# Issuing every second 4 MB load of the expert weights from ScalarE's DMA queue instead of SyncE's

## What is computed

```
logits = h @ w_router + b_router            # 256 x 32
top_val, top_idx = top_k(logits, 4); gates = softmax(top_val)
for each expert e, on the frames that chose it:
    hu  = xb @ w_up[e] + b_up[e]            # 1024 -> 2048
    act = min(glu, 7) * sigmoid(1.702 * min(glu, 7)) * (clip(lin, -7, 7) + 1)
    y   = (act @ w_down[e] + b_down[e]) * gate
x = x + sum over the chosen experts of y
```

## Time and profile before

| what | us |
|---|---|
| median of 3 executions | 1036.49 (1036.40 to 1037.47) |
| the profiled execution, its own time | 1035.9 |
| span of the profile | 1033.7 |
| PE busy | 997.6 (97%) |
| DVE / ACT / POOL busy | 202.8 / 114.4 / 12.8 |
| DMA | 424.94 MB, mean 411 GB/s |

### The profile page before, as it was taken

One profiled execution on the slowest core, in us unless ns is written; L12 is line 12 of the kernel. 1 busy time (PEld: TensorE's weight loads), 2 busy tenths in 40 slices (PEclk: granted clock), 3 DMA queues, 4 the chain that ended last, 5 costly groups with the idle time before them and its releaser, 6 DMA issues.

```text
span 1033.7 us, 10934 instructions
## 1 busy us (share of the span) xinstructions
PE 997.6 (97%) x4494; PEld 386.7 (37%) x4494; DVE 202.8 (20%) x486; ACT 114.4 (11%) x230; POOL 12.8 (1%) x26
## 2 busy tenths in 40 slices
PE   8999999999999999999999999899998989999998
PEld 4446553434343434333333334232333324232332
DVE  0456132121111211212121211112111211112012
ACT  2426111010000001010101000000000000000000
POOL 0200000000000000000000000000000000000000
PEclk9999999999999999999999999999999999999999
DMA  9955889999999999999999999999999999999996
GB/s 368 400 242 243 368 335 428 433 427 419 432 429 431 435 431 427 434 435 430 431 435 431 427 434 435 430 430 436 431 427 434 435 430 430 436 430 425 432 429 268
DMA packets 22609, 424.94 MB, mean 411 GB/s; under 512 B 3617, under 2 KB 4385, under 8 KB 6721
## 3 DMA queue, kind: packets, MB, share of 16 engines
q1 hardware_dynamic: 22208, 424.17, 96.4%
q10 hardware_dynamic: 384, 0.54, 0.1%
HBM read 423.65 MB, written 1.05 MB: 411 GB/s over the span
## 4 chain that ended last, share of the span: by engine, by line
PE 70%; DMA 28%; another core or an unknown queue 1%; DVE 0%; issue 0%; ACT 0%; POOLq 0%; SPq 0%; POOL 0%; DVEq 0%
PE psum L1433 31%; DMA everything<-in_w_moe 28%; PE psum L1467 15%; PE psum L1090 4%; PE psum L1314 4%; PE psum L1353 4%; PE psum L1223 3%; PE psum L1057 3%; PE psum L1304 2%; PE psum L1065 2%; PE psum L1082 1%; PE psum L1073 1%; PE psum L1362 0%; DMA everything<-in_x_turned 0%; PE psum L1325 0%
## 5 line engine op out<-in xcount | busy, mean ns | idle before, releaser
L1433 PE MATMUL psum<-everything 128*64 128x512 f32 x2048 | 463.7, 598 | 3.6 <-DMA everything<-in_w_moe 3.4
L1467 PE MATMUL psum<-everything 128*64 128x512 f32 x1024 | 227.8, 595 | 22.5 <-DMA everything<-in_w_moe 22.5
L1433 PEld LDWEIGHTS psum<-everything 128*64 128x64 f32 x2048 | 137.9, 136 | 297.3 <-issue 286.4
L1467 PEld LDWEIGHTS psum<-everything 128*64 128x64 f32 x1024 | 72.2, 137 | 164.9 <-issue 148.9
L736 DVE TENSOR_TENSOR everything<-psum,everything 128x512 f32<-128x512 f32 (+1 forms) x38 | 25.0, 663 | 342.8 <-PE psum L1314 332.5
L1022 DVE TENSOR_SCALAR everything<-psum 128x512 f32<-128x512 f32 x32 | 22.1, 692 | 344.9 <-PE psum L1433 344.9
L1314 PEld LDWEIGHTS psum<-everything 128*128 128x128 f32 x480 | 55.8, 191 | 24.3 <-issue 24.3
L1353 PE MATMUL psum<-everything 128*128 128x512 f32 x128 | 64.2, 606 | 0.0
L693 ACT ACTIVATE everything<-everything 128x512 f32<-128x512 f32 x32 | 20.2, 631 | 390.4 <-DVE everything L1022 390.4
L1314 PE MATMUL psum<-everything 128*128 128x128 f32 x480 | 61.5, 281 | 0.0
L1090 PE MATMUL psum<-everything 128*128 128x512 f32 x96 | 42.1, 594 | 0.0
(11 more groups left out here) (158 smaller groups left out, 296.4 us busy)
## 6 DMA issues: line engine op xcount, KB each, us to landing
everything<-in_w_moe SPq DMA_DIRECT2D x80, 4096.0 KB, 43.0
everything<-in_w_moe SPq DMA_DIRECT2D x27, 2048.0 KB, 15.6
everything<-in_w_moe SPq DMA_DIRECT2D x8, 1024.0 KB, 8.4
everything<-in_w_in SPq DMA_DIRECT2D x3, 2048.0 KB, 26.0
everything<-in_w_out SPq DMA_DIRECT2D x2, 2048.0 KB, 10.1
everything<-in_w_mem_kv SPq DMA_DIRECT2D x1, 2048.0 KB, 17.2
everything<-in_w_moe SPq DMA_DIRECT2D x4, 512.0 KB, 36.5
everything<-in_w_in SPq DMA_DIRECT2D x1, 1024.0 KB, 8.3
```

The costliest lines, as they stand in the source:

```text
L1433: mm = pe.matmul(psum[r:r + SLOTS, bank], XT[:, k, r:r + SLOTS], weights[i][:, column:column + N], start=k == 0 and not first, stop=k == K ...
L1467: mm = pe.matmul(psum[r:r + SLOTS, DOWN_BANKS[n]], actT[:, 2 * i + k, r:r + SLOTS], slot[:, column:column + N], start=i == 0 and k == 0, s ...
```

## The change

In the loop over pairs 2 to 13 SyncE begins only d0, d2 and d4. The transfers d1, d3 and d5 of these pairs are begun by ScalarE, one pair earlier in its own program: d1 behind the sigmoid of the first half, d3 behind that of the second half, d5 behind the last copy of Y. Each comes behind a wait of ScalarE for the same count of `slot_used` as SyncE waited for. SyncE still counts the stand-in semaphores. Pairs 0, 1, 14 and 15 are loaded by SyncE as before. Destinations, sizes and semaphores of the transfers are the same.

```diff
-            def pair(q, p):
+            def pair(q, p, odd=True):
                 for d in range(TWOS):
-                    wait_used(q, 2 * d + 1)
-                    sp.dma_start(two_slots[d], two_chunks(p * TWOS + d)).then_inc(two_in[d], 16)
+                    if odd or d % 2 == 0:
+                        wait_used(q, 2 * d + 1)
+                        sp.dma_start(two_slots[d], two_chunks(p * TWOS + d)).then_inc(two_in[d], 16)
                     credit(d)
...
             with sp.Fori(2, PAIRS - 2) as q:
-                pair(q, q)
+                pair(q, q, odd=False)
...
+            def next_two(q, d):
+                act.wait_ge(slot_used, q * PAIR_CHUNKS + (MIX_CHUNKS + 2 * d + 2))
+                act.dma_start(two_slots[d], w_moe[bass.ds((q + 1) * TWOS + d, 1)].rearrange("o r c -> (o r) c")
+                              ).then_inc(two_in[d], 16)
+
-            def pair(q, bdown=False):
+            def pair(q, bdown=False, loads=False):
                 for i in range(2):
                     act.wait_ge(glu_ready, 2 * q + (i + 1))
                     nc.scalar.activation(sig, glu, ACT.Sigmoid, scale=ALPHA).then_inc(sig_ready, 1)
+                    if loads:
+                        next_two(q, 2 * i + 1)
...
                     nc.scalar.activation(Y[:, n * N:(n + 1) * N], psum[:, DOWN_BANKS[n]], ACT.Copy).then_inc(y_ready, 1)
+                if loads:
+                    next_two(q, TWOS - 1)
...
             pair(0)
-            pair(1, bdown=True)
-            with act.Fori(2, PAIRS) as q:
+            pair(1, bdown=True, loads=True)
+            with act.Fori(2, PAIRS - 3) as q:
+                pair(q, loads=True)
+            with act.Fori(PAIRS - 3, PAIRS) as q:
                 pair(q)
```

## The result

The changed kernel takes 1057.97 us (1056.89 to 1058.70), the kernel before 1036.49: a ratio of 1.0201 (95% interval 1.0188 to 1.0214), 21.5 us slower. That is inside the range of 1031 to 1080 and outside the forecast's own, 1035 to 1039. The profiled execution has a span of 1055.6 us, against 1033.7.

A forecast was written before the change was run, and what follows sets the result against it. The prediction took the DMA engines as the bound; its terms 0 + 0 + 0.75 + 0 gave +0.75 us on 1036.5, so 1037.2 us, no measurable difference. The range was 1031 to 1080, the forecast's own 1035 to 1039.

The forecast's parts named there:

- What bounds the kernel: Whole loop: the DMA engines are the bound at 432 GB/s, 9.71 us per 4 MB transfer, although TensorE is 97% busy.
- 5 us at the very start: At d5's issue on ScalarE: over 40 us of transfers are queued ahead, but only 5 at the loop's very start.
- Added on ScalarE: 36 issues with waits in ScalarE's program, 0.317 us each: cover 7 us behind d1, about 3 behind d3; cost 0.
- The late last transfer: d5 of pair 13 lands 4.86 us late; TensorE's later waits make up 4.11, leaving +0.75 us.
- Rival 2: Last ScalarE transfer late by up to a whole one: +5.6 us, 1042; decides above 6.2 us of lateness; chance 0.11.
- The rate with two queues: Shared stretch of the loop: two queues of large transfers keep the DMA rate, 431 to 432 GB/s; effect 0.
- Rival 1: Shared stretch: two full queues disturb each other, 1055 to 1080 us by loss per transfer, 1102 by rate; chance 0.22.
- Rival 3: Shared stretch: one queue's packets fill what another leaves open, up to 436 GB/s, giving 1030 us; chance 0.12.
- SyncE's saved issues: 36 of SyncE's 72 issues removed, 0.333 us each, hidden below transfers already queued: gain 0.
- ScalarE's own time: ScalarE's added issues in the loop, 0.317 us each, fit before its next duties without delaying TensorE: cost 0.

The follow-up runs named there:

- the run that starts at pair 3: The changed kernel, except that ScalarE begins d1, d3 and d5 only of pairs 3 to 13 and SyncE loads all of pair 2: 1040.05 us, ratio 1.0031.
- the run with the added wait: The kernel before with one TensorE wait added ahead of pair 4, for d3 of that pair: 1038.33 us against 1036.94, ratio 1.0016.

## Why the prediction was right or wrong

**What bounds the kernel** was read rightly, and it is what makes the result understandable: time is lost where the DMA stream has too little to do, and a wait of TensorE costs what it takes from the stream. The text also had the number that matters, "5 us at the very start".

**The failed step is d3's, under "Added on ScalarE".** It asked what stands behind each issue, and for d3 it named "the next duty of ScalarE, the second copy of the activations". In pair 1 another one comes first, the issue of `b_down`, and there the question is not only which instruction stands behind but also which transfer stands behind on the queue. The entry read 0. It is 18.3 us of waiting for `b_down` and, with the half clock behind the wait, 18.8 us of stream. The rows to see it by were all there. I used the 8.3 us of `b_down` as evidence that queues share, in which it overtook SyncE's transfers, and did not ask what became of it once its own queue held 4 MB transfers. The wait could have been estimated: d1 lands at about 230, d3 at half speed 19.4 us later, at 249, and `b_down` behind it is needed at 237.

**The late last transfer** was right in kind and undersized: 0.75 us was put in, 3.6 and 3.5 were measured between the pairs of runs that end with pair 13 and pair 12 (1040.05 to 1036.45, 1040.14 to 1036.68). The lateness was taken as 4.86, half an interval, and was 6.1, as the two queues did not take turns evenly; and a drop of the granted clock behind the wait, 1.4 to 1.7 us, was not in the sum. This drop does not always come: with `b_down` ahead of d3 the 32 matmuls behind the last such wait, of 3.17 us, took 7.09, and the time was the same, as the stream itself ended 2.1 us later than in the kernel before and not 1.0, as in the run that starts at pair 3. Why it did was not followed up. Rival 2 had this mechanism, with a deciding point at 6.2.

**The rate with two queues**, taken as unchanged, was right: 432 GB/s before and after. Rival 1, 0.22 of the chance and the reason why the range reached 1080, was wrong: two full queues of large transfers show no dip. Rival 3 was wrong as well, as no run was measurably faster. So it is luck that the range held the result, by the price of a mechanism that did not act, and the chance of 0.33 for slower was too low because no case had the one that did. By the Trainium skill, page "DMA: Bandwidth & Descriptors", section "Issuing engines are not separate DMA queues", all queues interleave on the same engines and a second one saves only issue time. The rates agree, 432 GB/s with one queue and with two.

**SyncE's saved issues** (0) and **ScalarE's own time** (0) were right. Its 36 issues took about 0.35 us each and none was held up. One lag was larger than the 0.5 us put down for d5: in pair 1 slot 11 is free at 264.0 and ScalarE begins d5 at 266.05, as the copy of Y ahead of it waits for the matmuls of `b_down`.

## What to carry to other kernels

In these runs `b_down` never landed ahead of the 4 MB transfer begun before it on its queue: 255.2 behind 250.5, and on SyncE's queue 246.9 behind 246.0 and 256.0 behind 255.7. When large transfers are moved to a queue, list every other transfer on that queue, however small it may be, with the time at which it is needed: a 128 KB load that landed after 8 us with no large transfer ahead of it on its queue took 27 behind a 4 MB one. Where the DMA stream is the bound, weigh a wait by what is queued at that moment: 11 us of waiting cost 1.4 with a deep queue and 9.6 us cost 10.6 with a shallow one. If a queue is to be handed loads, hand them over where the ring has a lead, and take them back a pair before the end; here even this gained nothing.

## What was not expected of the hardware

Two queues of 4 MB transfers, in rows of 32 KB, move as much as one: 432 GB/s at a share of 1.00 in both. TensorE's granted clock went to 0.50, the level of 1.2 GHz, during waits of 9.6, 11.3 and 18.3 us, and the `b_down` matmuls and the chunk behind those of 9.6 and 18.3 us took 4.1 and 3.1 us more than usual. Behind a wait of 2.93 us it dropped at one place and not at another in the same execution: with that wait at chunk 10 the 32 matmuls took 8.78 us in pair 13 of the run that starts at pair 3, and 7.09 in pair 12. Behind the 1.98 us waits of the kernel before 16 matmuls took their usual 3.65; behind waits of the same length in the run with the added wait they took 5.35.
